# Three 1024-wide input projections as seven half-size products each, in a decoder block on one core

## The reference

```
h = rms_norm(x, g_mix)                       # x: 512 x 1024
z = h @ w_in                                 # 1024 x 4800
u, v, q_lat, kv_lat, k_rope, gate_a, gate_b = split(z)   # 1024, 1024, 384, 256, 64, 1024, 1024
v = layer_norm(gelu(v), ln_g, ln_b)
y_a = gelu(u) * (tril(w_s) applied to v in chunks of 128 positions + b)
y_b = mla_attention(rms_norm(q_lat), rms_norm(kv_lat), k_rope, ...)
x = x + (sigmoid(gate_a) * y_a + sigmoid(gate_b) * y_b) @ w_o
x = x + moe(rms_norm(x))                     # 64 experts, 8 for a token, one shared expert
x = x + sigmoid(rms_norm(x) @ w_ple_gate) * rms_norm(p @ w_ple_proj)
```

## Time and profile before

| what | value |
|---|---|
| runs | 1113.02, 1110.62, 1111.32 us; median 1111.32 us |
| the profiled execution | 1110.49 us, its span 1108.7 us, granted clock 1.0 |
| TensorE busy | 1092.9 us, 99% of the span |
| VectorE, ScalarE, GpSimd busy | 861.2, 787.0, 423.6 us |
| DMA | 291.60 MB, mean 263 GB/s |

### The profile page before, as it was taken

How to read it: one execution, slowest core, us unless ns; L and a number is a source line. 1 busy time by engine, 2 the same in 40 slices (tenths; PEclk the granted TensorE clock), 3 DMA queues, 4 the chain that set the end, 5 groups by cost and what they waited for, 6 DMA issues and landing times.

```text
span 1108.7 us, 17836 instructions
## 1 busy us (share of the span) xinstructions
PE 1092.9 (99%) x5488; PEld 914.7 (83%) x5488; DVE 861.2 (78%) x1239; ACT 787.0 (71%) x1270; POOL 423.6 (38%) x477
## 2 busy tenths in 40 slices
PE   7999999999999999999999999999999999999998
PEld 7988888878778888888888888888888888888787
DVE  4535532278765468999999999999999999999865
ACT  6644433357654343888888898889888988888772
POOL 1120000015276003355556555555655555555400
PEclk9999999999999999999999999999999999999999
DMA  7422422112402259999999999999999999999632
GB/s 251 153 76 76 142 85 76 29 57 71 158 1 71 101 225 381 356 377 382 394 393 388 391 393 388 391 391 393 395 396 396 396 394 393 392 393 359 192 151 76
DMA packets 72130, 291.60 MB, mean 263 GB/s; under 512 B 15187, under 2 KB 20598, under 8 KB 47126
## 3 DMA queue, kind: packets, MB, share of 16 engines
q1 hardware_dynamic: 52672, 254.13, 57.3%
q0 software_dynamic: 18768, 34.79, 12.5%
q10 hardware_dynamic: 646, 2.12, 0.5%
HBM read 284.61 MB, written 42.07 MB: 295 GB/s over the span
## 4 chain that ended last, share of the span: by engine, by line
PE 93%; DVE 3%; ACT 2%; POOL 1%; issue 1%; DMA 0%; ACTq 0%; POOLq 0%; DVEq 0%
PE bank L2065 11%; PE bank L2067 11%; PE bank L2066 11%; PE bank L1752 7%; PE bank L1789 6%; PE bank L1793 6%; PE bank L1790 6%; PE bank L2093 5%; PE bank L2091 5%; PE bank L2092 5%; PE bank L2030 5%; PE bank L1743 2%; PE bank L1944 1%; PE bank L2163 1%; PE bank L2165 1%; PE bank L2164 1%
## 5 line engine op out<-in xcount | busy, mean ns | idle before, releaser
L1624 DVE TENSOR_TENSOR arena_r<-arena,win_r 128x1024 fp32r<-128x1024 f32 x252 | 292.0, 1221 | 21.9 <-ACT win_r L1082 19.1
L1082 ACT ACTIVATE win_r<-arena 128x1024 fp32r<-128x1024 f32 x252 | 246.5, 1069 | 0.5 <-DMA resid<-in_w_exp_up 0.5
L2065 PE MATMUL bank<-win_r,work_r 128*128 128x512 f32 x512 | 206.5, 403 | 0.6 <-issue 0.6
L2066 PE MATMUL bank<-win_r,x_low_r 128*128 128x512 f32 x512 | 199.5, 390 | 0.0
L2067 PE MATMUL bank<-arena_r,work_r 128*128 128x512 f32 x504 | 197.4, 392 | 0.0
L1604 DVE TENSOR_TENSOR arena_r<-arena,hT_r 128x1024 fp32r<-128x1024 f32 x128 | 150.5, 1217 | 0.5 <-ACT hT_r L1090 0.5
L733 POOL DMA_INDIRECT moe_sum<-ya,sidx x64 | 111.5, 1743 | 102.7 <-ACT ya L1118 86.0
L1789 PE MATMUL bank<-arena_r,hT_r 128*128 128x512 f32 (+2 forms) x320 | 121.9, 381 | 2.2 <-DVE win_r L1222 2.1
L1790 PE MATMUL bank<-arena_r 128*128 128x512 f32 (+2 forms) x320 | 121.1, 378 | 0.0
L1793 PE MATMUL bank<-win_r,hT_r 128*128 128x512 f32 (+2 forms) x320 | 121.0, 378 | 0.0
L2067 PEld LDWEIGHTS bank<-arena_r,work_r 128*128 128x128 f32 x504 | 94.6, 188 | 21.7
(11 more groups left out here) (321 smaller groups left out, 2213.4 us busy)
## 6 DMA issues: line engine op xcount, KB each, us to landing
arena<-in_w_exp_down SPq DMA_DIRECT2D x64, 1024.0 KB
arena<-in_w_exp_gate SPq DMA_DIRECT2D x63, 1024.0 KB
arena<-in_w_exp_up SPq DMA_DIRECT2D x63, 1024.0 KB
win<-in_w_in SPq DMA_DIRECT2D x8, 2048.0 KB, 7.8
win<-in_w_o SPq DMA_DIRECT2D x2, 2048.0 KB, 7.9
arena<-in_w_ple_gate SPq DMA_DIRECT2D x2, 2048.0 KB, 13.7
arena<-moe_sum SPq DMA_DIRECT2D x7, 512.0 KB, 7.0
win<-in_mla_w_qb SPq DMA_DIRECT2D x4, 576.0 KB, 4.0
```

Source lines behind the costliest of these rows:

```text
L1082: act.activation(gu_hi[n % 2][:, :, cols], raw[:, :, cols], ACT.Copy).then_inc(gu_hi_r, 1)
L1624: dve.tensor_tensor(low_[:, :, cols], raw[:, :, cols], gu_hi[n % 2][:, :, cols].bitcast(F32), ALU.subtract).then_inc(gu_lo_r, 1)
L2065: pe.matmul(b_, x_hi[:, k, :], w_hi, start=(k == 0), stop=False)
L2066: pe.matmul(b_, x_lo[:, k, :], w_hi, start=False, stop=False)
```

## The change

Chunks 2 to 7 are no longer computed chunk by chunk. For v, u and gate_a in turn (p = 0, 1, 2) the 512 x 1024 by 1024 x 1024 product is cut into quarters: rows in two halves of 256 tokens, the inner dimension in halves of 512, columns in halves of 512. Seven products of quarters stand in place of eight (the method of Strassen in the form with few additions). Each is of 256 tokens by 512 by 512. In order they are called 11, T1, T2, 21, 22, T3, T4.

- The row sides S1 to S4 are sums and differences of quarters of the transposed rows. VectorE computes them once (`rows_1` to `rows_4`), each also gets a high and a low part, and all three p use them. So the gain is now multiplied into the rows and not into the weights.
- The weight sides T1 to T4 are sums of weight quarters: T1 is 11 + 12, T2 is T1 + 22, T4 is T2 + 21, T3 is 12 + 22. They are summed by an adding DMA of GpSimd (`add_weights`), 128 partitions x 4 blocks x 512 columns, 1 MB each, onto a quarter that SyncE has loaded plainly. T2 is added onto the buffer of T1, once VectorE has made T1's low part.
- VectorE adds the products together out of PSUM (`add_products`, 14 operations of 128 x 512 for each p). ScalarE copies product 11 out and applies gelu or sigmoid afterwards, from SBUF to SBUF. The products of gate_a are summed in the buffer of x (`resid`) and in `work`, and x is loaded again from HBM afterwards.
- The angles, the norm of the latents and the statistics and norm of v stand behind the last product of gate_a and u. Chunks 8 and 9 run as before, behind the products. The load of the layer norm's gain and bias stands ahead of chunk 8's load, behind a wait for product 22 of gate_a.
- At the start, `hT_evac` and `h_evac` work in pieces of 128 x 128, since each has its own gain, and the transposes of row tiles 2 and 3 both stand in the second tile of chunk 0.

```diff
+        HK, HT = KD // 2, SEQ // 2
...
-        hst = [arena[:, o_sigb + i * D:o_sigb + (i + 1) * D] for i in range(4)]
+        hst = [arena[:, o_qT + i * D:o_qT + (i + 1) * D] for i in range(4)]
...
+        NP = 3
+        in_res0, in_res1 = in_res
+        B_RAW = [{"11": in_ya[0], "T1": in_res0, "T2": in_res0, "21": in_w0[1], "22": in_w0[0], "T3": in_ya[1], "T4": in_res0}]
+        B_RAW += [{"11": in_w0[1], "T1": in_res[p % 2], "T2": in_res[p % 2], "21": in_w0[0], "22": in_w1[1], "T3": in_w1[0],
+                   "T4": in_res[p % 2]} for p in range(1, NP)]
...
+        S_AT = {"S1": ((arena, arena_r), o_sigb, arena_r, o_sigb + D), "S2": ((arena, arena_r), o_sigb + 2 * D, arena_r, o_sigb + 3 * D),
+                "S3": ((rope_q_, rope_q_r), 0, x_low_r, 0), "S4": ((work, work_r), 0, work_r, D)}
...
+        PRODUCTS = ("11", "T1", "T2", "21", "22", "T3", "T4")
+        PRODUCT_ROW = {"T1": "S1", "T2": "S2", "22": "S4", "T3": "S3"}
+        PRODUCT_BANK = {"11": 0, "T1": 4, "T2": 2, "21": 6, "22": 0, "T3": 4, "T4": 6}
...
+        LOWS = [("11", "S1", "T1", "S2", "T2", "S3", "S4", "21", "22", "T3", "T4")] + [("T1", "11", "T2", "21", "22", "T3", "T4")] * (NP - 1)
...
+        def half_chunk(p, name):
+            c = (OFF_V, OFF_U, OFF_GA)[p] + (512 if name[1] == "2" else 0)
+            k0 = (0 if name[0] == "1" else HK) * P
+            return w_in[k0:k0 + HK * P, c:c + 512].rearrange("(k p) n -> p k n", p=P)
...
+            def pairs_loads():
+                sp.wait_ge(tr_done, 2 * NT)
+                sp.wait_ge(rms_sq, NT)
+                half_load(v2(xr_, 0, HK, 512), half_chunk(0, "11"), ld_w0[0], 32)
+                half_load(v2(xr_, 2 * D, HK, 512), half_chunk(1, "11"), ld_w0[0], 48)
+                free(0)
+                half_load(v2(win0, 0, HK, 512), half_chunk(0, "22"), win_ready[0], 32)
+                half_load(v2(win0, 2 * D, HK, 512), half_chunk(0, "21"), win_ready[1], 32)
...
+                sp.wait_ge(pj_done, products_done(NP - 1, "22"))
                 sp.dma_start(lng, bc(a["sgu_ln_g"][0], D)).then_inc(ld_ln, 16)
                 sp.dma_start(lnb, bc(a["sgu_ln_b"][0], D)).then_inc(ld_ln, 16)
...
+            sp.wait_ge(pj_done, products_done(NP - 1, "T4"))
+            sp.wait_ge(lat_n, 3)
+            for t in range(NT):
+                rows_of_x(t)
...
+            def add_weights(p, name):
+                done, n = landed(p, name)
+                if n > 16:
+                    pool.wait_ge(done, n - 16)
+                base = {"T1": (ld_w0[0], 32 + 16 * p), "T3": (ld_w0[1], 32 + 16 * p)}.get(name)
+                if base is not None:
+                    pool.wait_ge(*base)
+                else:
+                    pool.wait_ge(lo_ready, split_count(LOWS, p, "T1" if name == "T2" else "T2"))
+                dst = (v2(ya_, 2 * D, HK, 512) if p == 0 else v2(win1, 0, HK, 512)) if name == "T3" else v2(xr_, p % 2 * 2 * D, HK, 512)
+                pool.dma_start(dst, half_chunk(p, {"T1": "12", "T2": "22", "T3": "22", "T4": "21"}[name]),
+                               accum_op=ALU.add).then_inc(done, 16)
+            add_weights(0, "T1")
+            add_weights(0, "T3")
+            add_weights(1, "T1")
+            add_weights(0, "T2")
+            add_weights(1, "T3")
+            add_weights(0, "T4")
...
+            def first_product_out(p):
+                act.wait_ge(pj_done, products_done(p, "11"))
+                for i in range(2):
+                    act.activation(quad_place(p, "12", i), bank[i][:, :], ACT.Copy).then_inc(pj_free[i], 2)
...
+            high_part(0, "11")
+            high_part(0, "S1")
+            evac(1, 0)
+            high_part(0, "S2")
+            high_part(0, "T1")
...
+            high_part(0, "T2")
+            high_part(0, "21")
+            first_product_out(0)
+            high_part(0, "22", products_done(0, "T1"))
+            high_part(0, "T3", products_done(0, "T2"))
+            high_part(0, "T4", products_done(0, "T2"))
...
+                    if w == FIRST and t == 0:
+                        act.wait_ge(z_ms, 3)
+                        act.activation(ssl, msl, ACT.Sqrt).then_inc(z_rt, 1)
...
+            def rows_1():
+                for i in range(2):
+                    dve.wait_ge(tr_free[i], NT)
+                link(dve.tensor_tensor(S1, row_hi(lower, second), row_hi(upper, second), ALU.subtract))
+                link(lower_lo(S1, second, ALU.add))
+                dve.tensor_tensor(S1, S1, row_lo(0, second), ALU.subtract).then_inc(combined, 1)
...
+            rows_1()
             split(1)
+            rows_2()
+            low_part(0, "11")
+            low_part(0, "S1")
+            low_part(0, "T1")
+            rows_3()
+            rows_4()
+            low_part(0, "S2")
...
+            low_part(0, "T2")
+            low_part(0, "S3")
+            low_part(0, "S4")
+            low_part(0, "21")
+            low_part(0, "22")
+            for p in range(NP):
+                add_products(p, "X")
+                add_products(p, "Y")
+                low_part(p, "T3")
+                low_part(p, "T4")
+                add_products(p, "11")
+                if p == 2:
+                    gated_quad("11")
+                add_products(p, "12")
+                if p + 1 < NP:
+                    low_part(p + 1, "T1", products_done(p, "22"))
+                add_products(p, "22")
+                add_products(p, "W")
+                if p + 1 < NP:
+                    low_part(p + 1, "11")
+                else:
+                    split(FIRST, range(HK))
+                    split(FIRST, range(HK, KD))
+                if p == 2:
+                    gated_quad("12")
+                add_products(p, "21")
+                if p + 1 < NP:
+                    low_part(p + 1, "T2", products_done(p + 1, "11"))
+                    low_part(p + 1, "21")
+                    low_part(p + 1, "22")
+            if NP == 3:
+                gated_quad("22")
+                gated_quad("21")
...
+            for i, n in enumerate((QL, KVL, ROPE)):
+                mean(msl[:, i * NT:(i + 1) * NT], ssl[:, i * NT:(i + 1) * NT], n, EPS).then_inc(z_ms, 1)
...
+                    if name == "11":
+                        pe.wait_ge(pj_free[i], 2 + 2 * p)
+                        if p:
+                            added(p - 1, "12", i)
+                    elif name == "T1":
+                        if p:
+                            added(p - 1, "W", i)
+                        else:
+                            pe.wait_ge(tr_free[i], NT)
+                    elif name == "T2":
+                        pe.wait_ge(pj_free[2 + i], 2 + 2 * p)
+                    elif name == "21":
+                        if p:
+                            added(p - 1, "21", i)
+                        else:
+                            pe.wait_ge(cols_ready, 3)
+                    elif name == "22":
+                        pe.wait_ge(pj_free[i], 4 + 2 * p)
+                    elif name == "T3":
+                        added(p, "Y", i)
+                    else:
+                        added(p, "11", i)
+                    for k in range(HK):
+                        if i == 0 and k % 2 == 0:
+                            pe.wait_ge(lo_ready, split_count(LOWS, p, name, k // 2))
...
+                        pe.matmul(b_, a_hi, w_hi, start=(k == 0), stop=False)
+                        pe.matmul(b_, a_lo, w_hi, start=False, stop=False)
+                        last = pe.matmul(b_, a_hi, w_lo, start=False, stop=(k == HK - 1))
+                last.then_inc(pj_done, 2 if name == "T4" else 1)
+            for p in range(NP):
+                for name in PRODUCTS:
+                    product(p, name)
+            pe.wait_ge(sum_read, 12 * (NP - 1) + SUM_READ["12"] + 2)
```

More of the change, by code:

```diff
@@ new lines, in rows_3, with rows_4 @@
+            def rows_3():
+                link(dve.tensor_tensor(S3, row_hi(upper, first), row_hi(upper, second), ALU.subtract))
+                link(dve.tensor_tensor(S3, S3, row_lo(0, first), ALU.add))
+                dve.tensor_tensor(S3, S3, row_lo(0, second), ALU.subtract).then_inc(combined, 1)
+            def rows_4():
+                dve.wait_ge(combined, 2)
+                link(dve.tensor_tensor(S4, S2, row_hi(lower, first), ALU.subtract))
+                lower_lo(S4, first, ALU.subtract).then_inc(combined, 1)
@@ new lines, in low_part @@
+            def low_part(p, name, room=None):
+                if room is not None:
+                    dve.wait_ge(pj_done, room)
+                if name[0] == "S":
+                    dve.wait_ge(hi_ready, split_count(HIGHS, p, name))
+                    dve.tensor_tensor(s_lo[name], s_raw[name], s_hi[name].bitcast(F32), ALU.subtract).then_inc(lo_ready, 1)
+                    return
+                for part in range(2):
+                    dve.wait_ge(hi_ready, split_count(HIGHS, p, name, part))
```

(3 more changed lines are left out.)

374 lines of the change are left out of this document (287 added, 87 removed).

## The result

| | before | changed |
|---|---|---|
| median (range), us | 1112.17 (1110.62 to 1113.42) | 1130.4 (1126.8 to 1132.32) |
| ratio, 95% interval | | 1.0161 (1.0131 to 1.019) |
| profiled execution, us | 1110.49 | 1126.8 |
| its span, us | 1108.7 | 1124.7 |
| granted clock | 1.00 | 0.989 |

The changed kernel is 1.6% slower: 18 us, where I had forecast 3 us less.

What follows compares the result with a forecast made beforehand. TensorE was taken to set the time alone. The terms -16.3 + 0.5 + 1.5 + 5 + 3.3 + 3.6 = -2.4 us, from 1110.49 profiled or the 1111.32 median, gave a forecast of 1108.5 us, range 1100 to 1122.

Steps and rivals of the forecast that it cites:

- The saving: Products in place of chunks 2 to 7: 504 matmuls instead of 576, 72 x 0.2267 = 16.3 us gained.
- The steady stage: Products of each p: VectorE (26.8 us) and ScalarE (21.7) keep up with 38.1 us; 0.5 us charged, at worst 3.
- All later sums have a slot or more to spare even at 7.8: Weight sums after the start: no wait even at 7.8 us a quarter, four being 31 us of 38.1.
- what would make me wrong in kind: Waits inside the products of p = 1 and 2, or a slower attention behind; no size given.
- The start: Longer evacuations and `rows_1` ahead of chunk 1: products start near 46.4 instead of 44.9 us, 1.5 us lost (0 to 4).
- The adding DMA: First products of v: T2 lands late at 4.2 us a quarter (3.0 to 7.8), 5 us lost.
- My own formula: T2 of v's landing: from 31.9 us, 6.4 plain loads, 16.8 adding, about 3 later loads, 1.2 semaphore: near 59.3 us.
- Rival (a): Adding DMA is dear, 5.5 to 7.8 us a quarter, T2 10 to 20 us late: 1113 to 1125 us; chance 25%.
- Rival (b): TensorE's clock slows after its new waits, about 2 us each, 2 to 6 added: 1111 to 1114 us; chance 15%.
- Chunk 8: Ahead of chunk 8: its load lands 11.4 us after product 22 of gate_a; 3.3 us lost (2 to 6).
- Chunk 9: Ahead of chunk 9: VectorE's list of 26.7 us delays its low parts; 3.6 us lost (2 to 6).
- The attention behind: After the projection: no term charged; a slower attention would make the prediction wrong in kind.

Runs made afterwards that it cites:

- e13: e11 with the tail edits of e6 (chunk 8's load ahead of gain and bias, chunk 9's low parts between v's statistics): 1097.1 us, 0.9886 against the kernel before.
- e2: The changed kernel with T2 of gate_a put ahead of its T3 in GpSimd's list: 1119.9 us, 1.0089 against the kernel before.
- e6: The changed kernel with chunk 8's load ahead of gain and bias, and chunk 9's low parts between v's statistics: 1120.9 us, 1.0094 against before.
- e7: The changed kernel with product T1 of v's 24 matmuls made three times over, to fill TensorE's wait: 1126.9 us, 1.0149 against before.
- e4: The changed kernel with GpSimd's twelve adding DMAs made plain copies (wrong weight sides, only time counts): 1112.9 us, 1.0017 against before.
- e5: The changed kernel with GpSimd's whole list of weight sums in the order of need: 1112.2 us, 1.0014 against before.
- e11: e5 with two waits on SyncE that hold plain loads back until T1 and T2 of v have landed: 1104.7 us, 0.9954 against before.
- e10: The changed kernel with list in order of need, T3 of v held for T2, early loads moved, tail edits, plain loads held back: 1108.6 us.

## Why the prediction was wrong, point by point

- **The saving.** Right: 72 x 0.2267 = 16.3 us. e13, which has nearly all other terms at nothing, gets 14.0 of it.
- **The steady stage.** Of VectorE and ScalarE, right: in u nothing waits, and in e13 nothing waits over 0.3 us in any of the three. "All later sums have a slot or more to spare even at 7.8" was false, and it is one of the two failed steps, the order of GpSimd's list; the other is the price of adding, below. I had counted engine time (31 of 38 us), not GpSimd's order: T3 of gate_a waits for a plain load that SyncE may issue only after product T3 of u, and T2 of gate_a, needed sooner, was behind it. I had named a wait inside p = 2 as what would make me wrong in kind. It cost 6.65 + 1.9 us; e2 took it away.
- **The start.** Sized at 1.5 us, with the products at 46.4. Measured 1.0 in the profiled execution, and 1.8 in e13, with the products at 46.49. A wait I had not listed came with it in other executions: chunk 1's second row tile is drained behind T1's high part (2.0 us in e6, 1.7 in e7).
- **The adding DMA.** This is the term that turned the sign. "4.2 is my value, nearer to the loaded row": it is 5.96, and a copy in the same place 2.90 where I had taken 2.6. My own formula, 31.9 + 6.4 + 4 x 5.96 + 3 + 1.2, gives 66.3 us for T2's landing; measured 67.6. That the two meet is partly luck. With copies at 2.90 the same formula gives 54.1, and e4 measured 59.3; and with T2 second in the list and the full price T2 landed at 59.8 (e5). The formula adds up the engines' work and leaves out that T1 of u waits for T3 to land, so that T2 is not even issued before 54.57 us. So the price failed (5.96 for 4.2), and beside it the same omission as above, a wait in GpSimd's list that I had put at nothing. The mean of the two bounds I had (3.0 and 7.8) would have been 5.4. The lower end rested on a guess, that scattered gathers cost twice a plain MB; the 5.7 that the same row gives with gathers at the plain price was all but right, and I had moved away from it. The wait came to 13.3 us and 1.4 of clock, against 5.
- **Rival (a)**, to which I gave 25%, is what happened in kind, from 5.5 us a quarter up as I had put it. Its 1113 to 1125 was too low: 1130.4 holds the wait at T2 of gate_a and the half clock besides, which it did not have. The Trainium skill, Collectives: The Full Stack, section The bandwidth ceiling: the fold count and why AG ≠ RS ≠ AR, has a reduce at about half a copy's rate; e4 agrees, 2.90 against 5.96. With the 5.2 us worked out from it I had a loss near 8 us and kept 5.
- **Rival (b)** was true as well, and not instead: three half-clock stretches of 1.4 to 1.9 us, 5.0 in all, where I had said about 2 each. I had made a rival of what came behind every wait of 4 us and more in these runs; in the forecast itself, with three waits of 3 to 5 us, this term was due. Behind chunk 9's 1.9 us wait it was 0.3. The Trainium skill, TensorE: Matmul & The Clock Gate, section HAM oscillation — how this bites in real kernels, has the half clock come back in gaps in which TensorE waits for DMA; this trace agrees, with 0.50 granted from 60 to 70 us.
- **Chunk 8.** Predicted 3.3, measured 4.2 (and 1.7 of clock). The load landed at 185.43, 12.5 us after the first issue behind product 22 (172.94), where I had counted 11.4.
- **Chunk 9.** Predicted 3.6, measured 1.9. The list of VectorE is right item by item (its first low part starts 25.3 us after chunk 8's first, where I had counted 25.5); chunk 8 itself ran 1.7 us longer on the half clock, which hid that much.
- **The attention behind** is unchanged, as said: spans and transposes differ by the same within 0.6 us.

The profiled execution is 18.7 us above the 1108.1 of my sum: 8.3 at T2 of v, 6.8 at T2 of gate_a, 5.3 of clock and 1.0 at chunk 8, less 1.6 at chunk 9 and 1.0 at the start and the steady stage, are 18.8. The range ended at 1122, below even rival (a)'s own 1125, although it was meant to hold most of (a) with (b): T2 of gate_a stood in no rival, and (b) was charged for waits of 3 to 5 us only.

## What to carry to other kernels

Work moved from an engine that sets the time to DMA needs a budget of the DMA engines by itself, with a measured price for each kind of transfer, and a date for each landing: here with the same twelve sums the kernel was 18 us slower or 13 faster, by the order of one list, two waits that hold plain loads back, and a tail put in another order. Count an in-order queue by its entries' own waits, each with what stands behind it, and repeat that for every round of a loop, since the first round being safe says nothing of the third. And where a forecast has waits of several us on TensorE, add the half clock behind each to the sum: here it was 1.4 to 1.9 us behind each of the waits of 4.2 us and more.

## What the runs showed of the hardware

- Adding a quarter (1 MB in rows of 2 KB) from HBM into SBUF takes the DMA engines 5.96 us, a copy 2.90; twelve have 6336 packets against 3264. Alone it landed 8.9 us after its issue, beside one other adding DMA and plain loads up to 21.9.
- With the list in the order of need, T1 of v took 14.3 us to land beside two plain quarters (e5) and 9.9 with them held back (e11). The two waits on SyncE that hold them back were worth 7.5 us (6.7 by the ratios).
- The granted clock read 0.50 while TensorE was idle from 60 to 70 us, and behind waits of 13.3, 6.65 and 4.2 us five to seven distances of 0.43 us between matmuls followed, the half level. Behind 1.7 us none did (e7). In between, the length of the wait alone does not tell: behind 3.40 us none did (e10, 81.95 us), behind 3.29 us five did (e7, 186.27 us).
